# Two parts of the second layer's modulation accumulated on GpSimd during the dense feed-forward

## The reference

```python
for l in range(DEPTH):                                   # DEPTH = 2
    ms = jnp.split(jax.nn.silu(c) @ ada_w[l] + ada_b[l], 6, axis=-1)
    mc = jnp.split(jax.nn.silu(c_ctx) @ ada_w[l] + ada_b[l], 6, axis=-1)
    ...                                                  # token mixing, shift ms[0], scale ms[1], gate ms[2]
    f_lat = modulate(rmsnorm(x_lat, pre_ffn_g[l]), ms[3], ms[4])
    y_lat = swiglu(f_lat, w1, w3, w2)                    # l = 0: dense, width 2816
    # l = 1: moe_swiglu, top 2 of 8 experts of width 3584
    x_lat = x_lat + ms[5] * rmsnorm(y_lat, post_ffn_g[l])
```

## Time and profile before

| | us |
|---|---|
| median of three runs | 1877.4 (1876.48 to 1880.33) |
| the profiled execution | 1876.53 |
| its span | 1874.7 |
| TensorE busy in the span | 1726.1 (92%) |
| VectorE busy | 1415.7 (76%) |
| ScalarE busy | 1099.6 (59%) |
| GpSimd busy | 71.1 (4%) |

### The profile page before, as it was taken

How to read it: one execution, slowest core, us unless ns; L and a number is a source line. 1 busy time by engine, 2 the same in 40 slices (tenths; PEclk the granted TensorE clock), 3 DMA queues, 4 the chain that set the end, 5 groups by cost and what they waited for, 6 DMA issues and landing times.

```text
span 1874.7 us, 24261 instructions
## 1 busy us (share of the span) xinstructions
PE 1726.1 (92%) x8008; PEld 1397.5 (75%) x8008; DVE 1415.7 (76%) x1647; ACT 1099.6 (59%) x1409; POOL 71.1 (4%) x91
## 2 busy tenths in 40 slices
PE   6998798999999969874999999999999999999993
PEld 3765586878878858564888888888888888888883
DVE  3846647565754487653899999999999999999994
ACT  3334534222222253543788888888888888888883
POOL 0110300000010000121000000000000000000000
PEclk9999998999999989986999999999999999999997
DMA  9945134655674427243899999999999999999992
GB/s 321 254 129 182 55 127 128 220 197 186 212 228 139 159 64 277 83 146 102 315 383 362 395 374 374 392 352 396 378 369 392 356 391 382 366 394 358 387 379 89
DMA packets 229520, 505.78 MB, mean 270 GB/s; under 512 B 16377, under 2 KB 47249, under 8 KB 229185
## 3 DMA queue, kind: packets, MB, share of 16 engines
q1 hardware_dynamic: 225216, 493.30, 73.5%
q0 software_dynamic: 4224, 11.47, 2.4%
HBM read 497.34 MB, written 19.96 MB: 276 GB/s over the span
## 4 chain that ended last, share of the span: by engine, by line
issue 54%; PE 34%; DVE 7%; ACT 3%; DMA 2%; SPq 0%; POOL 0%; POOLq 0%; ACTq 0%; DVEq 0%
PE ps L600 10%; PE ps L602 10%; PE ps L601 10%; DVE w_lo L1371 1%; DMA raw<-in_ffn_w 1%; PE ps L833 1%; DVE att L1624 1%; PE ps L669 1%; DMA raw<-in_ada_w 1%; DVE xs L1550 1%; ACT w_hi L1072 1%; DVE hT_lo L1523 1%; ACT pr L1189 0%; PE ps L797 0%; PE ps L821 0%
## 5 line engine op out<-in xcount | busy, mean ns | idle before, releaser
L1371 DVE TENSOR_TENSOR w_lo<-raw,w_hi 128x1024 fp32r<-128x1024 f32 x570 | 684.9, 1222 | 208.3 <-ACT w_hi L1072 174.0
L1283 ACT ACTIVATE w_hi<-raw 128x1024 fp32r<-128x1024 f32 x448 | 473.9, 1062 | 105.9 <-PE ps L602 105.9
L600 PE MATMUL ps<-w_hi,he_hi 128*128 128x512 f32 x896 | 354.4, 396 | 0.7 <-DVE he_lo L1773 0.7
L602 PE MATMUL ps<-w_hi,he_lo 128*128 128x512 f32 x896 | 350.1, 391 | 0.0
L601 PE MATMUL ps<-w_lo,he_hi 128*128 128x512 f32 x896 | 349.6, 390 | 0.0
L1371 DVE TENSOR_TENSOR w_lo<-raw_more,w_hi 128x1024 fp32r<-128x1024 f32 x224 | 273.9, 1225 | 45.7 <-ACT w_hi L1283 26.2
L1283 ACT ACTIVATE w_hi<-raw_more 128x1024 fp32r<-128x1024 f32 x224 | 237.7, 1062 | 53.5 <-PE ps L602 53.5
L1072 ACT ACTIVATE w_hi<-raw 128x1024 fp32r<-128x1024 f32 x122 | 128.6, 1063 | 215.1 <-PE ps L602 190.2
L602 PEld LDWEIGHTS ps<-w_hi,he_lo 128*128 128x128 f32 x896 | 168.6, 188 | 36.0
L600 PEld LDWEIGHTS ps<-w_hi,he_hi 128*128 128x128 f32 x896 | 168.7, 188 | 34.9 <-issue 1.0
L601 PEld LDWEIGHTS ps<-w_lo,he_hi 128*128 128x128 f32 x896 | 168.8, 188 | 33.9
(11 more groups left out here) (229 smaller groups left out, 2002.9 us busy)
## 6 DMA issues: line engine op xcount, KB each, us to landing
raw<-in_moe_w SPq DMA_DIRECT2D x448, 512.0 KB, 6.0
raw_more<-in_moe_w SPq DMA_DIRECT2D x224, 512.0 KB, 6.0
raw<-in_ada_w SPq DMA_DIRECT2D x96, 512.0 KB, 4.7
raw<-in_ffn_w SPq DMA_DIRECT2D x66, 512.0 KB, 5.0
raw<-in_w_in SPq DMA_DIRECT2D x40, 512.0 KB, 6.7
raw<-in_w_out SPq DMA_DIRECT2D x16, 512.0 KB, 4.6
yrows<-in_x SPq DMA_DIRECT2D x8, 512.0 KB, 7.6
xe<-xrows SPq DMA_DIRECT2D x8, 512.0 KB, 6.4
```

The source lines that it names most:

```text
L600: pe.matmul(o, lh, rh, start=start, stop=False)
L602: return pe.matmul(o, ll, rh, start=False, stop=stop)
L1283: act.activation(w_hi[:, s % SPL, :], expert_raw(i), ACT.Copy).then_inc(hi_done, 1)
L1371: dve.tensor_tensor(w_lo[:, s_ % SPL, :], src, w_hi[:, s_ % SPL, :].bitcast(F32), ALU.subtract)\
```

## The change

Parts 4 and 5 go from VectorE to GpSimd. Their sixteen units get a kind of their own ("p"), and their places in the list are spread: part 4 behind weight units 2, 4, 8, 12, 16, 20, 24 and 28, part 5 behind 41, 43, 45, 47, 49, 51, 53 and 55, one each. For the first unit of a part GpSimd writes raw times scalar straight into a row of `gg` (row 0 for part 4, row 1 for part 5); for the other seven it multiplies the raw slot in place and then adds it to the row, two instructions with a wait between them. SyncE waits for `pool acc` before it reuses such a slot. In GpSimd's list `pool_part(0)` stands ahead of `gate_rows(1)` and `pool_part(1)` behind `gate_params(2)`.

```diff
-FFN_ACC = {**{i: 1 for i in (*range(4, 12), *range(20, 28), *range(32, 40))}, **{i: 2 for i in (*range(44, 48), *range(56, 60))}}
+FFN_ACC = {i: 1 for i in (*range(4, 12), *range(20, 28), *range(32, 40))}
+POOL_PARTS = (4, 5)
+POOL_ACC = (2, 4, 8, 12, 16, 20, 24, 28, 41, 43, 45, 47, 49, 51, 53, 55)
...
                         sp.wait_ge(sg("acc"), acc_count(o))
+                    elif o.pool:
+                        sp.wait_ge(sg("pool acc"), o.p + 1)
...
+            def pool_part(n):
+
+                for u in at["acc", POOL_PARTS[n]]:
+                    pool.wait_ge(raw_in[u.k % RAW], raw_count(u.k))
+                    k, total = u.p % KD, gg[:, n, :]
+                    if k == 0:
+                        pool.tensor_scalar(total, raw_at(u.k), cstat[:, k, 0:1], None, ALU.mult).then_inc(sg("pool acc"), 1)
+                    else:
+                        link(pool.tensor_scalar(raw_at(u.k), raw_at(u.k), cstat[:, k, 0:1], None, ALU.mult))
+                        pool.wait_ge(sg("pool acc"), u.p)
+                        pool.tensor_tensor(total, total, raw_at(u.k), ALU.add).then_inc(sg("pool acc"), 1)
...
             layer_norm_params(1)
+            pool.wait_ge(sg("z pm0"), 2 * NB)
+            pool_part(0)
             gate_rows(1)
             gate_params(2)
+            pool_part(1)
             pool.wait_ge(sg("mod fin"), len(MODS))
...
-                pe.wait_ge(sg("acc"), acc_end[i])
+                if i in POOL_PARTS:
+                    pe.wait_ge(sg("pool acc"), KD * (POOL_PARTS.index(i) + 1))
+                else:
+                    pe.wait_ge(sg("acc"), acc_end[i])
```

More of the change, by code:

```diff
@@ L53 @@
 FFN_SUM = {16: 1, 28: 2, 40: 3, 52: 4, 64: 5}
-FFN_ACC = {**{i: 1 for i in (*range(4, 12), *range(20, 28), *range(32, 40))}, **{i: 2 for i in (*range(44, 48), *range(56, 60))}}
+FFN_ACC = {i: 1 for i in (*range(4, 12), *range(20, 28), *range(32, 40))}
+POOL_PARTS = (4, 5)
+POOL_ACC = (2, 4, 8, 12, 16, 20, 24, 28, 41, 43, 45, 47, 49, 51, 53, 55)
+DVE_PARTS = [i for i in range(len(PARTS)) if i not in POOL_PARTS]
 GATE_STEP = 0
@@ L123, in __init__ @@
         self.k, self.src, self.shape = k, src, shape
-        self.split, self.acc = kind == "s", kind == "c"
+        self.split, self.acc, self.pool = kind == "s", kind == "c", kind == "p"
         self.s = n if kind == "s" else None
@@ L192, in plan_units @@
                             acc(FFN_ACC.get(i, 0))
+                            acc(POOL_ACC.count(i), "p")
                             i += 1
@@ L197, in plan_units @@
                         acc(FFN_ACC.get(i, 0))
+                        acc(POOL_ACC.count(i), "p")
                         i += 1
-    assert n["c"] == KD * len(PARTS)
+    assert n["c"] == KD * len(DVE_PARTS) and n["p"] == KD * len(POOL_PARTS)
     return units, at, n["s"], step_end
@@ L397, in turn_bank @@
             return ADA + 1 if c < 4 else bank
-        acc_end = [sum(KD * streams(i) for i in range(n + 1)) for n in range(len(PARTS))]
+        acc_end = {n: sum(KD * streams(i) for i in DVE_PARTS if i <= n) for n in DVE_PARTS}
         def acc_count(u):
-            i, k = u.c // KD, u.c % KD
-            return (acc_end[i - 1] if i else 0) + streams(i) * (k + 1)
+            i, k = DVE_PARTS[u.c // KD], u.c % KD
+            return acc_end[i] - streams(i) * (KD - 1 - k)
         gates_in = [32 * sum(streams(i) for i in GATES[:n + 1]) for n in range(len(GATES))]
@@ L651, in acc_sum @@
                         q = 2 * half + r
+                        total = gg[:, POOL_PARTS.index(i)] if i in POOL_PARTS else acc[:, acc_row(i, r)]
                         m = pe.matmul(ps[32 * q:32 * q + 32, bank, :], ones[:, 0:32],
-                                      acc[:, acc_row(i, r), 512 * half:512 * half + 512], start=True, stop=True,
+                                      total[:, 512 * half:512 * half + 512], start=True, stop=True,
                                       tile_position=(0, 32 * q))
@@ L1404, in split_upto @@
                 k = split_units[min(s, stage_end[0])].k + 1
-                while k < len(units) and units[k].acc:
+                while k < len(units) and (units[k].acc or units[k].pool):
                     k += 1
```

13 lines of the change are left out of this document (7 added, 6 removed).

## The result

| | before | after |
|---|---|---|
| median of 22 runs, us | 1876.84 | 1880.72 |
| the profiled execution | 1876.53 | 1880.82 |
| its span | 1874.7 | 1878.7 |

The ratio is 1.0018, with a 95% interval of 1.0011 to 1.0025: the changed kernel is slower by a little, 3.9 us on the medians, which is just inside what the prediction had called no measurable change (0.2%). The forecast was 1880.0 with a range of 1875.2 to 1886.0. The number came out; the parts that it was made of did not all do so, and that is what the experiments are about.

What follows compares the result with a forecast made beforehand. The prediction took TensorE to bound the feed-forward, with 3.7 us of waits for VectorE's sums. Adding 1.3 (load 48), 0.6 (its split) and 1.0 (second group), +2.9 us on 1876.53, it forecast 1880.0 us, range 1875.2 to 1886.0.

Steps and rivals of the forecast that it cites:

- What bounds the stage: Feed-forward: TensorE bounds it and waits for VectorE's sums three times, 3.7 us in all, the most any offload could save.
- The longest wait: TensorE's 2.75 us stall at weight unit 46 is for unit 48's 16.44 us load behind copies, not for VectorE's arithmetic.
- The gate row: Part 3's row on VectorE: ready at 530.4 instead of 532.4, as two additions ahead of it go.
- The late load of unit 47: Load waits for part 5's first GpSimd instruction; unit 48 then lands at 554.8, and unit 46's stall grows by 1.3 us.
- the split of 48: VectorE's split of weight unit 48 beside part 5, held by a GpSimd addition: +0.6 us, 0 to 2.5.
- The second group: Split of unit 24 ahead of the left half's sums, delayed by a GpSimd addition: +1.0 us, 0 to 1.9.
- The head: Start of the feed-forward: its 10.9 us for `hT_lo` were called out of the change's reach, with no term in the sum.
- The sum: Whole program: +1.3 for load 48, +0.6 for its split, +1.0 for the second group, together +2.9 us.
- The exclusion rival: GpSimd and VectorE hold each other throughout, multiplies included: +1 to +2 us at three groups, about 1882.5; chance 0.15.
- the `at_lo` steps: VectorE steps in the feed-forward groups: forecast as covered by 2.6 us; waits for them would mean the exclusion.
- the forecast's own price for a multiply: GpSimd's TENSOR_SCALAR beside VectorE's two-input instructions: priced at no delay, against up to 2.5 us for a TENSOR_TENSOR.
- The four unheld instructions: Four two-input VectorE instructions beside GpSimd's TENSOR_SCALAR from 183.55, 0.28 us each, cited as evidence that multiplies hold nothing.

Runs made afterwards that it cites:

- The version with all three waits removed and nothing offloaded: Kernel before, all additions on VectorE, last copies moved to weight unit 52, modulation units behind 24 and 36 to 19 and 31; ratios 0.9980 and 0.9967 in two runs.
- the version with the offload: Changed kernel, GpSimd starting behind the last `hT_lo`, its units re-spaced, VectorE's units behind 24 and 36 moved to 19 and 31; 1873.7 us, ratio 0.9975.
- The run with the head alone: Changed kernel, with GpSimd starting part 4 only after VectorE has split all eight column blocks of the feed-forward's input; 1878.7 us, ratio 1.0006.
- the one with only the addition kept out: Changed kernel, with only GpSimd's first addition waiting for the split of the feed-forward's input, its two multiplies starting as before; ratio 0.9998.

## Why the prediction was right in its number and wrong in one of its steps

**What bounds the stage: right.** The feed-forward is TensorE's, and the pool for any offload was 3.7 us. The version with all three waits removed and nothing offloaded shows it: its stretch is 4.6 and 4.4 us shorter in two traces, the 3.7 us and some 0.25 us at the restart behind each of the three waits, and the version with the offload gets no more.

**The longest wait is a transfer's: right, and shown.** Moving the copies alone removes it; unit 48 lands in 6.4 us instead of 16.4.

**The gate row: right.** It was to be ready 2.0 us earlier, at 530.4 on the old time axis. It was ready at 533.66 + 0.70 = 534.36 in an execution in which TensorE's sum at weight unit 40 came 3.99 us later than before (523.87 against 519.88), which is 530.4 on the old axis.

**The late load of unit 47: right in its mechanism, too large by 2.9 us in its price.** Four terms were mis-sized, and all to the same side. GpSimd's DMA instructions took 542.25 - 534.64 = 7.6 us, not 8.86: the wait for the 2 KB writes to DRAM was 1.34 instead of 2.67 us, and what differs is the company. In the old order three 512 KB loads go out from 529.05 to 531.11, just ahead of the writes at 532.70, and a fourth with the copies from 535.48 on; in the new one the last load went out at 516.42, 18 us ahead. All four traces with part 4 behind units 44 to 47 on VectorE have 2.3 to 2.7 us there, the ten others 1.34. That the loads are the cause is likely and was not tested by itself. The multiply took 2.9 us, not 3.1. Unit 48 landed in 9.1 us, not 10. And the split of 48 was held 0.1 us, not 0.6. That is 1.2 + 0.2 + 0.9 + 0.5 = 2.8 of the difference between 4.7 and 1.8. The prediction took the duration of the DMA part from a row of the old order although it argued in the next paragraph that SyncE would be silent by then.

**The second group: right**, +1.2 us where +1.0 was forecast, with the mechanism that was named (a split of 3.08 us beside an addition).

**The head: the step that failed.** The sum has no term for it. The first part said of the wait for `hT_lo` that it lies at the head of the stage, "out of the change's reach". It was the largest single loss, 2.1 us, with 0.5 for `xn` beside it. The prediction looked for places without slack where GpSimd's *paced* work would pass by and overlooked the place where its work begins: the wait for `z pm0` releases it, with two units already in the ring, at exactly the moment when VectorE's serial work begins. The row of the new wait was in the diff; the question that was not asked is what else the engine that gives this release does next. The run with the head alone shows it, and the one with only the addition kept out splits it.

The half microsecond of `xn` could have been read in the trace of the kernel before. The prediction looked for VectorE's two-input instructions beside GpSimd and passed over a TENSOR_SCALAR that GpSimd's TENSOR_TENSOR from 185.72 to 186.99 holds there, shown here with the same line without GpSimd:

```profile
185.87 1.39 DVE L1618 TENSOR_SCALAR pr<-pr,att 128x512 f32<-128x512 f32 x1
204.67 0.49 DVE L1618 TENSOR_SCALAR pr<-pr,att 128x512 f32<-128x512 f32 x1
```

**The sum.** Measured against before in the named waits: +2.7 (head) + 1.2 (second group) - 1.0 (unit 46) = +2.9 us, the forecast's sum from other terms: 1.9 + 1.0. The right total is luck: an overlooked 2.7 against an overpriced 2.8. The spans differ by 4.0 us, 1.1 more than the waits. Laid beside each other matmul by matmul, the two traces show where. The changed kernel's execution is 0.3 us ahead at the head's first product (283.45 against 283.72), 2.4 behind at the feed-forward's first (297.26 against 294.87) and 2.8 behind after eighteen more, because the granted clock stays at its lower level, 1.2 GHz, to about 303.1 and not to 299.7, behind a TensorE wait of 8.1 us and not 6.0: another 0.4 us. It is 3.1 behind at the last wait of the feed-forward (662.34 against 659.28), 3.3 at TensorE's last matmul (1849.85 against 1846.57) and 4.0 at the end. So 2.9 us are in the named waits and 0.4 in the clock behind the head, less 0.3 from ahead of it; the last 0.9 come after the feed-forward, 0.7 of them behind the last matmul, in code that was not changed. What those 0.7 us are is open. From that last matmul to the end it takes 27.8 to 28.9 us in the traces of this study, so they may be no more than the difference between two executions.

**The exclusion rival: wrong as a rule, right in one half.** The multiplies do not hold VectorE's two-input instructions to their end, and the `at_lo` steps cost TensorE nothing. But the forecast's own price for a multiply, nothing, was too low as well: a split that starts at its beginning is held for 0.6 to 0.7 us. The four unheld instructions that it leaned on start 0.8 us into theirs (184.38 against 183.55); in the same trace line 1619, started at 199.42 and 0.3 us into a multiply, takes 1.15 us instead of 0.75. And an addition of GpSimd's is no isolated hit: in five of the traces two of VectorE's additions beside one take 4.6 to 5.5 us, alone 2.48.

## What to carry to other kernels

Before work is moved to an idle engine, find out what the busy one is waited for: here the longest wait that bore VectorE's name was a 16 us load behind copies, and one line in SyncE's order was worth more than 19 us of arithmetic. An engine whose instructions hold another's, as GpSimd's held VectorE's here, is not idle capacity; what matters is when it runs, and its start deserves the closest look, because the semaphore that frees it often fires where the other engine's serial work begins. And a wait of an in-order queue on a newly employed engine is priced by everything that stands in that engine's list ahead of it, durations taken for the new company and not the old.

## What the runs showed of the hardware

- GpSimd's TENSOR_TENSOR of 128 x 1024 in fp32 took 2.4 us where nothing held it and a TENSOR_SCALAR with one operation 2.85 us. The row of half the size with two operations (2.08) had bounded the latter at 2.1 to 4.2.
- A GpSimd TENSOR_TENSOR held a VectorE TENSOR_TENSOR with two SBUF inputs to its end (2.71 instead of 0.69 us) and a VectorE TENSOR_SCALAR too (1.39 instead of 0.49).
- A GpSimd TENSOR_SCALAR held two-input VectorE instructions only in its first microsecond: splits that started 0.27 and 0.43 us into it took 1.93 and 1.82 us instead of 1.2, and an instruction that started 2.6 us into it took its usual 0.69. VectorE's TENSOR_SCALAR it held to its end (1.28 instead of 0.75).
- The load of 512 KB landed in 16.4 us right behind a pair of copies with GpSimd's broadcasts issued just behind it, in 9.1 us right behind the copies with the broadcasts issued some 7 to 9 us ahead of it, in 6.9 us 1.6 us behind the copies with no broadcasts, in 6.4 us with the broadcasts and no copies, and in 5.3 us 3.6 us behind the copies with no broadcasts.
